# Layer two's first weight loads: one slot handed back two products sooner, one load that waits for rows instead of their stores, one slot freed at the next turn

## The chip, the cores and the metric

The kernel runs on one NeuronCore of a Trainium2 chip. The metric is the device time of one execution in microseconds; the median of three runs is shown, and beside them stands one profiled execution with its trace.

## What is computed

Two layers of a decoder trunk on 520 tokens (512 of a prompt and 8 sampled ones) with a width of 1024, all in float32. Each layer is a mixer, a layer norm, a mixture of experts and another layer norm:

```
xp = layer_norm(ALPHA * xp + mixer(xp))      # layer one: short conv, layer two: RG-LRU
mp = hier_moe(xp, w_group, w_expert, w_gate[32], w_up[32], w_down[32])
xp = layer_norm(ALPHA * xp + mp)
# hier_moe: the best of 4 groups, the best 2 of its 8 experts for each token
hmid = silu(xb @ w_gate[e]) * (xb @ w_up[e]);  out = hmid @ w_down[e]
```

One expert has three weights of 1024 x 512 (2 MB each), so a layer reads 32 x 3 x 2 MB = 192 MB of expert weights.

## The kernel before

**The ring.** All weights pass through `ring`, ten slots of 2 MB. A load is called by its position; `ring_slot` gives its slot, `CYCLE` (line 104) the order of slots in an expert layer. SyncE (`block.sync`) issues all weight loads in the order of their positions, each once TensorE has freed its slot. TensorE says so by counting up one semaphore, `freed`: certain matmuls carry an increment, and because TensorE works in order, the start of such a matmul says that all before it are done. SyncE's `room(pos)` waits for a count. For the first ten loads of an expert layer the counts are written out in `ROOM` (line 106, one tuple for each layer), after that `freed_after` (line 154) gives them. The three slots of expert 0 are handed back in parts (`SPLIT`): the gate weights in two quarters and a half, the up and down weights in two halves.

**The end of the mixer, which the change touches.** The output projection is computed as a two-level sum with seven products for each of four column groups q, numbered i = 1 to 7 (`EARLY`, `LATE`, lines 116 and 117). The last order of them is (q,6), (q,7), (q,4) for q = 0 to 3, then (0,3), (0,2), (1,3), (1,2), (2,3), (2,2), (3,3), (3,2). A product is 4 matmuls in the program and 8 in the trace, since each float32 matmul shows as two. In layer two slot 5 holds the sums of tokens ("pieces") that products 4, 5, 6 and 7 read, slot 6 the copies, slot 7 the sums of weights that the products (q,3) read, slots 3 and 4 the output weights. Between the products stand short products for the router (`logits`, line 889).

In layer two `freed` goes up at product (1,3) (this one after a wait for `zT_done`), at (2,3) and at the last of `logits`. Load 5 (into slot 5) and load 6 wait for the first of these, load 7 for the second, load 8 and load 9 for the last.

**From the mixer to the experts.** Then the rows of tokens are turned and normalized: `turn_token` on TensorE, the scaling on ScalarE (line 1425), which counts up `xn_done` for each of five tiles of 104 tokens. Each tile is stored to `x1_dram`, three by ScalarE's queue (line 1418) and two by GpSimd's (line 666). Expert 0's rows are picked on TensorE from what is in SBUF. Expert 1's rows are gathered from `x1_dram` by an indirect DMA of GpSimd (line 675), which waits for all five stores (`x1_out`, `row_in`); it is the first of the gathers. Load 9 of layer two waits for the same five stores on SyncE (lines 528 and 529), and what SyncE has to issue after it is queued behind it.

**One expert on TensorE** (`expert`): the gate product (`project(0, ...)`), the up product (`project(1, ...)`), half of the turning of the next expert's rows (`turn_rows`, line 1060), the turning of the hidden rows, the other half, and the down product (`down`, line 1143). `project` with `free` counts up `freed` at its first matmul, and for expert 1 that signal frees the second half of expert 0's down slot. Expert 0 turns expert 1's rows (`next_rows(False)`) after its down product, in one piece, and then computes `destinations`.

Of the kernel before, what the change touches and what calls it, by code (L numbers as in the profile page):

```python
# [19 lines left out]
NT = T // TT  # L20
LAST = SEQ - (NT - 1) * TT
HALF = T // 2
DEPTH = 2
# [47 lines left out]
POS_EXP = (POS_OUT[0] + U_OUT, POS_OUT[1] + U_OUT)  # L71
# [14 lines left out]
SPLIT = [p + u for p in POS_EXP for u in range(3)]  # L86
# [16 lines left out]
DENSE = U_IN[0] + U_OUT  # L103
CYCLE = ((2, 3, 4, 5, 6, 7, 0, 1, 8, 9), (0, 1, 8, 9, 2, 5, 6, 3, 4, 7))
SCRATCH = ((0, 1), (5, 6, 7))
ROOM = ((6, 6, 6, 6, 6, 6, 8, 8, 9, 10), (1, 2, 3, 4, 5, 6, 6, 7, 8, 8))


def ring_slot(pos):

    if pos < DENSE:
        return pos
    l = int(pos >= POS_EXP[1])
    return CYCLE[l][(pos - POS_EXP[l]) % RING]
# [13 lines left out]
def late_at(n):  # L128

    return len(EARLY) + n  # L130
# [22 lines left out]

def freed_after(pos):

    return pos + 1 + sum(pos >= p for p in SPLIT) + sum(pos >= p for p in POS_EXP) + int(pos >= POS_EXP[1])


def gathered(e):
# [14 lines left out]
def room_count(pos):  # L174

    for l in range(DEPTH):
        if POS_EXP[l] <= pos < POS_EXP[l] + RING:
            return (0, freed_after(POS_IN[1] - 1))[l] + ROOM[l][pos - POS_EXP[l]]
    return freed_after(pos - RING)
# [7 lines left out]
def build(nc, a, outs):  # L187
    y_prompt, y_sample, na_p, na_s, nb_p, nb_s, nh_p, nh_s = outs
    with ExitStack() as ctx:
# [3 lines left out]
        def sem(name):  # L193
            return ctx.enter_context(nc.semaphore(name))
# [174 lines left out]
        row_in = sem("row_in")  # L369
# [14 lines left out]
        mm_gate = sem("mm_gate")  # L384
# [26 lines left out]
        xn_done = sem("xn_done")  # L411
        x1_out = sem("x1_out")
# [89 lines left out]
        def _(sp):  # L502
# [5 lines left out]
            def expert(l, pos, e):  # L508
                for u, w in enumerate((gates, ups, downs)):
                    s = ring_slot(pos + u)  # L510
                    if pos + u - RING in SPLIT:
                        half = KT * FE // 2
                        if pos + u - RING in POS_EXP:
                            sp.wait_ge(freed, freed_after(pos + u - RING) - 2)
                            sp.dma_start(ring[:, s, :half // 2], w[l][e][:, :half // 2]).then_inc(loaded[s], 16)
                            sp.wait_ge(freed, freed_after(pos + u - RING) - 1)
                            sp.dma_start(ring[:, s, half // 2:half], w[l][e][:, half // 2:half]).then_inc(loaded[s], 16)
                        else:
                            sp.wait_ge(freed, freed_after(pos + u - RING) - 1)
                            sp.dma_start(ring[:, s, :half], w[l][e][:, :half] if u < 2 else w[l][e][:, 0, :]  # L520
                                         ).then_inc(loaded[s], 16)
                        room(pos + u)
                        sp.dma_start(ring[:, s, half:], w[l][e][:, half:] if u < 2 else w[l][e][:, 1, :]
                                     ).then_inc(loaded[s], 16)
                        continue
                    room(pos + u)
                    if pos + u == POS_EXP[1] + RING - 1:
                        sp.wait_ge(x1_out, 16 * 2 * DEPTH)
                        sp.wait_ge(row_in, 16 * (13 + 3 * DEPTH))
                    out = ring[:, s, :] if u < 2 else ring[:, s, :].rearrange("p (h n) -> p h n", h=2)  # L530
                    if e == END and u > 0:
                        half = KT * FE // 2
                        first, second = ((w[l][e][:, :half], w[l][e][:, half:]) if u == 1
                                         else (w[l][e][:, 0, :], w[l][e][:, 1, :]))
                        sp.dma_start(ring[:, s, :half], first).then_inc((last_up, last_down)[u - 1], 16)
                        sp.dma_start(ring[:, s, half:], second).then_inc(loaded[s], 16)
                        continue
                    sp.dma_start(out, w[l][e]).then_inc(loaded[s], 16)
# [29 lines left out]
            for l in L:  # L568
# [4 lines left out]
                else:  # L573
# [3 lines left out]
                    pos = POS_IN[1] + KT // 2  # L577
# [6 lines left out]
                for u in range(U_OUT):  # L584
                    pos = POS_OUT[l] + u
# [18 lines left out]
                with sp.If(n_over > 0):  # L604
                    sp.wait_ge(y_mm[l], END)
                    with sp.Fori(0, n_over) as o:
                        sp.wait_ge(v_y[l], o + 1)
                        e = sp.value_load(over_i[0:1, bass.ds(o, 1)], min_val=0, max_val=NE - 1)
# [127 lines left out]
        def _(pe):  # L736
# [111 lines left out]
            for l in L:  # L848
# [30 lines left out]
                q = 2 * l  # L879
# [85 lines left out]
                for n in range(3, len(LATE)):  # L965
                    q, i = LATE[n]
                    bank_free(late_at(n))
                    late_sum(q, i)
                    free = 0
                    if (q, i) == (1, 3):  # L970
                        pe.wait_ge(zT_done, KT * l + KT // 2)
                        free = (2, 1)[l]
                    if (q, i) == (2, 3):
                        free = 1
                    out_product(l, q, i, late_at(n), free=free).then_inc(out_mm, 1)
                    if q and i == 7:
                        logits(q - 1)
                    if i == 2:
                        logits(KT // 2 + q - 1)
# [114 lines left out]
                def project(u, slot, free, first=False, split=False, halves=False):  # L1094

                    for k in range(KT):
                        if halves:
                            half_in(last_up, 1, k, KT)
                        if first and k == KT // 2:
                            row_numbers()  # L1100
                        if first and k in (0, 2):
                            pe.wait_ge(t_sb[l], k // 2 + 1)
                        if first and k == KT // 2:
                            pe.wait_ge(t_dve, l + 1)
                        for hf in range(2):
                            col = k * FE + hf * FH
                            mm = pe.matmul(ps[hf * ROWS:(hf + 1) * ROWS, (GATE_BANK, 3)[u], :FH],  # L1107
                                           xgT[:, k, :], ring[:, slot, col:col + FH],
                                           start=(k == 0), stop=(k == KT - 1))
                            if free and (k, hf) in (((1, 1), (KT // 2 - 1, 1)) if first else ((0, 0),)):  # L1110
                                mm.then_inc(freed, 1)
                            if split and (k, hf) == (KT // 2 - 1, 1):
                                mm.then_inc(freed, 1)
                    return mm
# [35 lines left out]
                def expert(e, sums_too=False):  # L1150

                    pos = POS_EXP[l] + 3 * e
                    slots = [ring_slot(pos + u) for u in range(3)]
                    if e > 0:
                        pe.wait_ge(t_sb[l], e + 2)
                    pe.wait_ge(loaded[slots[0]], load_target(pos))
                    project(0, slots[0], True, first=(e == 0)).then_inc(mm_gate, 1)
                    if e < END:
                        pe.wait_ge(loaded[slots[1]], load_target(pos + 1))
                    b = (e + 1) % IN_BUFS  # L1160
                    project(1, slots[1], True, split=(e == 0), halves=(e == END)).then_inc(gu_mm[l], 1)

                    def next_rows(free, ks=range(KT)):
                        pe.wait_ge(gath[IN_BUFS * l + b], gathered(e + 1))
                        turn_rows(xg[b], t_mm[l], free, ks)

                    if e + 1 in CHOSEN:
                        choose_rows(e + 1)
                    elif 0 < e < END:
                        next_rows(True, range(KT // 2))  # L1170
                    if sums_too:
                        overflow_rows()
                    if e == 0:
                        pe.wait_ge(idx_ok[l], 1)
                        state_rows()
                    pe.wait_ge(hid_ok[l], e + 1)
                    turn_hidden(h_mm[l], e in (0, END))
                    if e + 1 in CHOSEN:
                        turn_chosen(e + 1)
                    elif 0 < e < END:  # L1180
                        next_rows(False, range(KT // 2, KT))
                    if e < END:
                        pe.wait_ge(loaded[slots[2]], load_target(pos + 2))
                    pe.wait_ge(h_sb[l], e + 1)
                    pe.wait_ge(y_act[l], e)
                    down(slots[2], y_mm[l], split=(e == 0), halves=(e == END))
                    if e == 0:
                        pe.wait_ge(st_sb, 2 * (l + 1))
                        next_rows(False)
                        destinations()  # L1190

                def turn_end():
# [1039 lines left out]
```

## Time and profile before

| | us |
|---|---|
| median of 3 runs | 1406.62 |
| lowest and highest | 1405.63 and 1407.18 |
| profiled execution | 1409.14 |
| its span | 1407.4 |

| engine | busy us | share of the span |
|---|---|---|
| TensorE matmul | 1346.2 | 96% |
| TensorE weight load | 898.0 | 64% |
| VectorE | 546.6 | 39% |
| ScalarE | 220.0 | 16% |
| GpSimd | 122.2 | 9% |

The granted clock of TensorE is at its full level nearly throughout (0.996 of it as a mean). The DMA engines moved 472.88 MB with a mean of 336 GB/s. In the page's 40 slices of 35.2 us their busy share is 9 tenths and more from slice 8 to 19 and from slice 28 to 39, the two expert layers, and 1 to 3 tenths between them. A busy TensorE is not one at its peak, since ends of matmuls are modelled; a wait on a row is read from the bracket behind it, which has the idle time and what ended it.

### The profile page before, as it was taken

The page shows a single profiled execution, that of the slowest core. Times are in us where ns is not written, and L with a number is a line of the kernel's source. Part 1 is how long each engine was busy: PE and PEld are TensorE (multiplying, and loading weights), DVE is VectorE, ACT ScalarE, POOL GpSimd, SP SyncE. Part 2 cuts the span into 40 slices and gives each one's busy share as a digit, 9 for nine tenths or more (in the row PEclk, how much of TensorE's full clock was granted, in tenths as well). Part 3 has the DMA queues.
Part 4 walks back from the last instruction along what each step waited for, and adds up shares of the span by engine and source line. Part 5 has one row for each costly group of instructions (what it writes and reads, how often), then busy time and mean ns, then how long its engine had stood idle before and what let it go on. Part 6 is the DMA issues. An engine that isn't in the chain of part 4 may idle for free.

```text
span 1407.4 us, 20418 instructions
## 1 busy us (share of the span) xinstructions
PE 1346.2 (96%) x8720; PEld 898.0 (64%) x8720; DVE 546.6 (39%) x1163; ACT 220.0 (16%) x388; POOL 122.2 (9%) x138
## 2 busy tenths in 40 slices
PE   7999999999999999998899999999999999999886
PEld 6888876565555555664478888666555555566452
DVE  5667676322111121232255888652211111213117
ACT  1000014000101000100134444220000001010012
POOL 0000000101100010111010000010001100112100
PEclk9999999999999999999999999999999999999999
DMA  9930178999999999999994113689999999999995
GB/s 265 299 128 1 52 307 336 386 423 427 424 422 425 425 424 421 426 423 422 382 322 153 60 61 120 273 352 425 424 425 422 424 426 424 425 423 423 421 404 215
DMA packets 98892, 472.88 MB, mean 336 GB/s; under 512 B 16669, under 2 KB 51485, under 8 KB 64233
## 3 DMA queue, kind: packets, MB, share of 16 engines
q1 hardware_dynamic: 82797, 449.74, 79.0%
q0 software_dynamic: 11520, 15.52, 3.2%
q10 hardware_dynamic: 4484, 6.30, 1.6%
q8 instruction: 70, 1.15, 0.3%
q14 instruction: 21, 0.17, 0.0%
HBM read 468.77 MB, written 27.32 MB: 352 GB/s over the span
## 4 chain that ended last, share of the span: by engine, by line
PE 82%; DMA 13%; ACT 2%; DVE 2%; issue 1%; SPq 0%; POOL 0%; POOLq 0%; DVEq 0%
PE ps L1107 26%; PE ps L1143 14%; PE ps L799 10%; PE ps L740 9%; PE ps L843 7%; PE ps L1072 7%; DMA ring<-in_moe_w_down 3%; DMA ring<-in_moe_w_up 3%; DMA ring<-in_moe_w_gate 3%; PE ps L1060 3%; DMA yrows<-A,Bt 1%; PE ps L1083 1%; DMA ring<-in_a_w_in 1%; PE ps L1131 1%; PE ps L860 1%
## 5 line engine op out<-in xcount | busy, mean ns | idle before, releaser
L1107 PE MATMUL ps<-ring,A 128*64 128x256 f32 x4096 | 457.0, 380 | 20.1 <-DMA ring<-in_moe_w_up 8.6
L1107 PEld LDWEIGHTS ps<-ring,A 128*64 128x64 f32 x4096 | 324.7, 137 | 163.0 <-issue 43.4
L1143 PE MATMUL ps<-ring,A 128*64 128x512 f32 x1024 | 233.8, 597 | 8.1 <-DMA ring<-in_moe_w_down 1.5
L2077 DVE TENSOR_TENSOR A<-A,ps 128x256 f32<-128x256 f32 x64 | 26.9, 421 | 547.8 <-PE ps L1107 547.8
L1143 PEld LDWEIGHTS ps<-ring,A 128*64 128x64 f32 x1024 | 75.9, 136 | 120.5 <-issue 113.0
L740 PE MATMUL ps<-A,ring 128*128 128x260 f32 x576 | 130.6, 388 | 3.6 <-DMA ring<-in_a_w_in 3.6
L740 PEld LDWEIGHTS ps<-A,ring 128*128 128x128 f32 x576 | 111.2, 193 | 21.2 <-issue 3.8
L675 POOL DMA_INDIRECT A<-x,idx x42 | 44.5, 1060 | 678.7 <-PE ps L1060 628.9
L1072 PE MATMUL ps<-C,Bt 104*64 104x512 f32 x400 | 95.6, 620 | 0.0
L2080 DVE COPY A<-ps 128x256 f32<-128x256 f32 x64 | 27.1, 424 | 120.6 <-PE ps L1131 120.6
L1480 ACT ACTIVATE A<-ps 128x512 f32<-128x512 f32 x42 | 25.1, 597 | 307.2 <-PE ps L1143 307.2
L1072 PEld LDWEIGHTS ps<-C,Bt 104*64 104x64 f32 x400 | 34.1, 135 | 47.8 <-issue 46.1
L799 PE MATMUL ps<-A,ring 128*128 128x260 f32 x264 | 61.6, 382 | 0.0
L843 PE MATMUL ps<-ring 128*128 128x260 f32 x256 | 58.0, 385 | 0.0
L1060 PE MATMUL ps<-ident,A 128*128 128x128 f32 x336 | 55.2, 288 | 1.2 <-DMA A<-x,idx 1.2
L1060 PEld LDWEIGHTS ps<-ident,A 128*128 128x128 f32 x336 | 44.3, 195 | 18.3 <-issue 18.3
L1467 ACT ACTIVATE A<-ps 128x256 f32<-128x256 f32 x64 | 24.5, 383 | 200.2 <-PE ps L1107 198.0
L799 PEld LDWEIGHTS ps<-A,ring 128*128 128x128 f32 x264 | 50.2, 190 | 7.7
L843 PEld LDWEIGHTS ps<-ring 128*128 128x128 f32 x256 | 48.1, 190 | 9.6 <-issue 2.5
L682 POOL DMA_INDIRECT yrows<-A,Bt x42 | 44.3, 1055 | 91.6 <-ACT A L1480 83.6
L843 PE MATMUL ps<-Bt,ring 128*128 128x260 f32 x192 | 44.3, 386 | 0.0
L843 PEld LDWEIGHTS ps<-Bt,ring 128*128 128x128 f32 x192 | 36.0, 190 | 7.7 <-issue 2.5
(300 smaller groups left out, 1160.2 us busy)
## 6 DMA issues: line engine op xcount, KB each, us to landing
ring<-in_moe_w_gate SPq DMA_DIRECT2D x62, 2048.0 KB, 25.9
ring<-in_moe_w_up SPq DMA_DIRECT2D x60, 2048.0 KB, 25.7
ring<-in_moe_w_down SPq DMA_DIRECT2D x60, 2048.0 KB, 29.0
ring<-in_a_w_in SPq DMA_DIRECT2D x24, 512.0 KB, 7.6
ring<-yrows SPq DMA_DIRECT2D x10, 1024.0 KB, 9.1
ring<-in_moe_w_down SPq DMA_DIRECT2D x8, 1024.0 KB, 35.8
ring<-in_b_w_in SPq DMA_DIRECT2D x8, 1024.0 KB, 12.8
ring<-in_moe_w_up SPq DMA_DIRECT2D x6, 1024.0 KB, 37.7
```

The costliest lines, as they stand in the source:

```text
L675: pool.indirect_dma_start(out=xg[e % IN_BUFS], out_offset=None, in_=x1_dram[l], in_offset=bass.IndirectOffsetOnAxis(ap=idx[:, e:e + 1], ax ...
L682: pool.indirect_dma_start(out=half_rows, out_offset=bass.IndirectOffsetOnAxis(ap=where, axis=0), in_=rows, in_offset=None, bounds_check=2 ...
L740: mm = pe.matmul(bank, lhs(k), rhs(k), start=(k == 0), stop=(k == KT - 1))
L799: mm = pe.matmul(ps[:, part_bank(u, i), :HALF], w[:, k, :], x[i][:, k, :] if i in x else pieces[4 * t[i] + k], start=(k == 0), stop=(k == ...
L843: mm = pe.matmul(ps[:, out_bank(l, g), :HALF], w[:, k, :], x(k), start=(k == 0), stop=(k == KH - 1))
L1060: mm = pe.transpose(ps[:, k // 4, (k % 4) * P:(k % 4 + 1) * P], xv[:, k, :], ident[:, :])
L1072: mm = pe.matmul(ps[h * ROWS:(h + 1) * ROWS, 7, :], slots1[:, i, :], xv[:, h], start=(i == 0), stop=(i == NT - 1))
L1107: mm = pe.matmul(ps[hf * ROWS:(hf + 1) * ROWS, (GATE_BANK, 3)[u], :FH], xgT[:, k, :], ring[:, slot, col:col + FH], start=(k == 0), stop=(k ...
L1143: mm = pe.matmul(ps[nh * ROWS:(nh + 1) * ROWS, 2, :], hidT[:, at:at + ROWS], ring[:, slot, m * D + nh * 512:m * D + (nh + 1) * 512], start ...
L1480: act.activation(yo[j], ps[:, 2, :], ACT.Copy).then_inc(y_act[l], 1)
L2077: tt(gated, gated, ps[:, 3, :FH], ALU.mult).then_inc(ready, 1)
L2080: dve.tensor_copy(hidT, ps[:, 4, :FT * ROWS]).then_inc(ready, 1)
```

## The change

It moves signals and waits, and adds or removes no computation and no transfer.

1. In layer two, product (0,3) counts up `freed` as well. The counts of `ROOM` behind it and `freed_after` go up by one, so that load 5 waits for (0,3) and all others for what they waited for.
2. Load 9 of layer two waits until all five tiles are normalized in that layer (`xn_done` at 15) instead of for their stores.
3. In both layers, expert 1's gate product no longer counts up `freed`; the first transpose of expert 1's rows, at the end of expert 0, does.

```diff
-ROOM = ((6, 6, 6, 6, 6, 6, 8, 8, 9, 10), (1, 2, 3, 4, 5, 6, 6, 7, 8, 8))
+ROOM = ((6, 6, 6, 6, 6, 6, 8, 8, 9, 10), (1, 2, 3, 4, 5, 6, 7, 8, 9, 9))
...
-    return pos + 1 + sum(pos >= p for p in SPLIT) + sum(pos >= p for p in POS_EXP) + int(pos >= POS_EXP[1])
+    return pos + 1 + sum(pos >= p for p in SPLIT) + sum(pos >= p for p in POS_EXP) + 2 * int(pos >= POS_EXP[1])
...
                     if pos + u == POS_EXP[1] + RING - 1:
-                        sp.wait_ge(x1_out, 16 * 2 * DEPTH)
-                        sp.wait_ge(row_in, 16 * (13 + 3 * DEPTH))
+                        sp.wait_ge(xn_done, NT * (2 * DEPTH - 1))
...
-                    if (q, i) == (2, 3):
+                    if (q, i) == (2, 3) or (l, q, i) == (1, 0, 3):
                         free = 1
...
-                    project(0, slots[0], True, first=(e == 0)).then_inc(mm_gate, 1)
+                    project(0, slots[0], e != 1, first=(e == 0)).then_inc(mm_gate, 1)
...
                     if e == 0:
                         pe.wait_ge(st_sb, 2 * (l + 1))
-                        next_rows(False)
+                        next_rows(True)
                         destinations()
```

## Rows read from the trace of the kernel before

**Rows 1.** The chain of waits: start us, us, what
```profile
630.55 42.39 DMA ring<-in_moe_w_up
...
1264.41 36.79 DMA ring<-in_moe_w_gate
1301.20 42.65 DMA ring<-in_moe_w_down
...
1373.38 7.05 DMA ring<-yrows
```

**Rows 2.** Stretches: us, busy of each engine, clock, DMA share, GB/s
```profile
910.00:913.00 3.00, 3.00 (x14) 0.92 (x16) 2.69 (x10) 2.07 (x2) 0.57 (x1) 1.00 0.92 313
913.00:916.00 3.00, 2.92 (x18) 1.30 (x14) 2.23 (x8) 0.95 (x3) 0.00 (x0) 1.00 0.94 277
916.00:919.00 3.00, 2.45 (x52) 1.83 (x54) 2.87 (x9) 2.95 (x8) 0.00 (x0) 1.00 0.57 193
919.00:922.00 3.00, 3.00 (x43) 2.07 (x38) 2.65 (x14) 1.52 (x3) 0.12 (x1) 1.00 0.07 26
...
1020.00:1300.00 280.00, 276.14 (x1938) 162.59 (x1936) 57.34 (x104) 26.18 (x51) 34.81 (x33) 1.00 1.01 424
```

**Rows 3.** Timeline of SyncE's queue, layer two: start us, us, the issue
```profile
889.20 0.38 SPq L538 DMA_DIRECT2D ring<-in_moe_w_down  x1
...
902.03 0.38 SPq L538 DMA_DIRECT2D ring<-in_moe_w_down  x1
921.10 0.33 SPq L538 DMA_DIRECT2D ring<-in_moe_w_gate  x1
...
933.35 0.33 SPq L523 DMA_DIRECT2D ring<-in_moe_w_gate  x1
936.80 0.33 SPq L538 DMA_DIRECT2D ring<-in_moe_w_up  x1
```

**Rows 4.** Waits of SyncE's queue: us in total, times, longest us
```profile
SPq L529 <- DMA x<-C: 18.6, 1, 18.6
```

**Rows 5.** Issues at 936.80: count, KB, us to landing
```profile
ring<-in_moe_w_up SPq DMA_DIRECT2D x1, 2048.0 KB, 14.7
```

**Rows 6.** Issues at 260.78, the twin in layer one
```profile
ring<-in_moe_w_up SPq DMA_DIRECT2D x1, 2048.0 KB, 7.6
```

**Rows 7.** Timeline of TensorE, layer two: start us, us, group
```profile
884.30 3.67 PE L843 MATMUL ps<-Bt,ring 128*128 128x260 f32 x16
...
888.46 3.77 PE L843 MATMUL ps<-Bt,ring 128*128 128x260 f32 x16
...
929.97 1.13 PE L1060 MATMUL ps<-ident,A 128*128 128x128 f32 x8
...
932.67 7.13 PE L1107 MATMUL ps<-ring,A 128*64 128x256 f32 x64 [0.27 <-DVE A L2051]
```

**Rows 8.** DMA queues from 910 to 913: packets, MB, share of 16 engines
```profile
q10 hardware_dynamic: 132, 0.49, 44.6%
q1 hardware_dynamic: 45, 0.25, 25.1%
q0 software_dynamic: 64, 0.19, 21.2%
```

**Rows 9.** Timeline of ScalarE, the last tile normalized in layer two
```profile
910.86 1.22 ACT L1425 ACTIVATE C<-ps,stat 104x1024 f32<-104x1024 f32 x1
```

**Rows 10.** Issues of expert 1's gather in layer two, at 921.88
```profile
A<-x,idx POOLq DMA_INDIRECT x1, 8.0
```

**Rows 11.** Expert 1's gather in layer one, and TensorE behind it
```profile
A<-x,idx POOLq DMA_INDIRECT x1, 8.9
...
253.97 1.13 PE L1060 MATMUL ps<-ident,A 128*128 128x128 f32 x8 [1.24 <-DMA A<-x,idx]
```

**Rows 12.** Issue at 657.98 and its landing: layer one's last half
```profile
657.98 3.35 SPq L536 DMA_DIRECT2D ring<-in_moe_w_down  x1
...
ring<-in_moe_w_down SPq DMA_DIRECT2D x1, 1024.0 KB, 35.6
```

**Rows 13.** Issue at 1339.46 and its landing: layer two's last half
```profile
1339.46 4.41 SPq L536 DMA_DIRECT2D ring<-in_moe_w_down  x1
...
ring<-in_moe_w_down SPq DMA_DIRECT2D x1, 1024.0 KB, 36.0
```

**Rows 14.** The store of GpSimd's queue issued at 911.27
```profile
x<-C POOLq DMA_DIRECT2D x1, 416.0 KB, 9.3
```

## The prediction

> **What bounds the kernel now.** I read the chain of waits first. Each of the two expert layers ends in a stretch where TensorE is waiting for weights: "DMA ring<-in_moe_w_up" holds 42.39 us of layer one, and two weight loads hold 36.79 and 42.65 us of layer two, after which comes the fetch of the scattered rows [rows 1]. Then I read busy time and DMA by stretch: from 1020 to 1300 us the sixteen DMA engines are at 1.01 with 424 GB/s, and TensorE is at 276 of 280 us [rows 2]. So TensorE works off what the ring of ten slots holds until it meets the DMA stream, and the end of an expert layer comes when the last of 192 MB of weights has landed. A microsecond is won or lost only where that stream has a hole or fills one. In layer two the hole is at its start: the DMA share falls to 0.57 and 0.07 in 916 to 922 us [rows 2]. The issues on SyncE's queue and its waits say why: the tenth load of the ring goes out at 921.10, after an 18.6 us wait for the stores of the normalized rows [rows 3, 4]. From there the stream has a backlog. The second expert layer's load issued at 936.80 (expert 4's up weights; I call it load 13, counted from 0 in its layer) needs 14.7 us to land [rows 3, 5]; its twin in layer one, issued at 260.78, needs 7.6 us [rows 6]. The difference, 7.1 us, is the backlog in layer two at that point, and its most possible gain if every byte had moved earlier.
>
> The sums are made in the profiled execution (1409.14 us, span 1407.4); its own time is 2.5 us over the median of the three runs, and I carry the difference over to the median 1406.62.
>
> **Part 1, slot 5 handed back at product (0,3).** Load 5 goes out at 889.20, right after product (1,3) begins at 888.46; (0,3) begins at 884.30 [rows 3, 7]. So load 5 goes out near 885.0, 4.2 us sooner. Loads 6 and 7 keep their products, because the raised counts only take in the new signal. Load 8 waits for the last logits product and stays at 902.03 [rows 3]. Three loads at 424 GB/s [rows 2] take 3 x 4.95 us, so the first three are through at about 901 instead of 905, the queue runs empty, and load 8, issued at 902.03, has ended by about 908.5. TensorE waits for none of them. What the part brings is that the stores no longer share with the tail of load 8: SyncE's queue (q1) holds 25.1% of the engines in 910 to 913 [rows 8], which is 0.75 us of work. That is its whole worth to the stream.
>
> **Part 2, load 9 waits for the normalized rows, not for their stores.** ScalarE ends the last of them at 910.86 + 1.22 = 912.08 [rows 9], so load 9 goes out at about 912.2, 8.9 us sooner. If nothing else moved, it would fill the idle time of the DMA engines from 913 to 922, where the first bytes of the old load 9 flow: 0.06 x 3 + 0.43 x 3 + 0.93 x 3 = 4.3 us [rows 2], with the 0.75 us of part 1 5.0 us in all. That is the upper end.
> Against it stands what the old wait protected. The stores, 5 of 416 KB, are in their queues from 910 to 921, and expert 1's gather waits for the last: it goes out at 921.88, lands after 8.0 us at 929.9, and TensorE turns its rows at 929.97 with no idle time shown [rows 7, 10]. There is no slack. In layer one the gather lands late and TensorE idles 1.24 us [rows 11]. So each microsecond by which the last store lands later is one by which TensorE starts expert 1 later, and everything that TensorE frees afterwards (load 13's slot half-way through the up and gate products, and so on) is issued later by as much. Call it d. The trace shows no store beside a load of 16 KB rows, so I bound it. Load 9 is 2048 KB, 4.95 us of all engines. Off go 0.75 us (part 1), and up to 1.3 us of idle in 916 to 919 (0.43 x 3); on go the two quarters of load 10, which no longer stand behind load 9's issue and go out when project's first products free them, at about 917.6 and 918.5: 2 x 512 KB, 0 to 2.5 us of which come ahead of the last store. d lies between 4.95 - 0.75 - 1.3 = 2.9 and 4.95 - 0.75 + 2.5 = 6.7 us. I take the middle, 4.8, because half of the idle is a tail of few engines and half of the quarters should slip in.
> What d leaves: load 13 is issued at 936.80 + 4.8 = 941.6. Work ahead of it, counted from 913.3: loads 9 to 12, 19.8 us; stores left, 4.3 us; gathers and state rows, about 3.4 us (an estimate: from 922 to load 13's landing at 951.5 are 29.5 us, five loads are 24.75 of them, and 1.3 is half of what an unloaded load takes beyond its 4.95). That ends at 941, and load 13's bytes start 1.3 us after its issue, at 942.9, so there is no backlog left, and load 13 lands as its twin does, 7.6 us after issue, at 949.2: 2.3 us sooner than 951.5. In formula: gain at load 13 = 7.1 - d, at most 5.0. One more term: a stream that starts without backlog has small holes among its next loads. Layer one's, from load 13's landing at 268.4 to the last half at 657.98 + 35.6 = 693.6, takes 425.2 us; layer two's, from 951.5 to 1339.46 + 36.0 = 1375.5, takes 424.0 [rows 5, 6, 12, 13]. So 1.2 us is given back. Part 2 and 1 together: 7.1 - 4.8 - 1.2 = 1.1 us gained.
>
> **Part 3, the second half of expert 0's down slot freed at the next turn.** No instruction is added; the signal moves from expert 1's first gate product (932.67) to the first transpose of its rows (929.97) [rows 7], 2.7 us. On SyncE that one issue (933.35 [rows 3]) comes sooner and nothing is queued before it. The issue after it is unmoved, since load 13 waits for expert 1's up products. In layer two before, 7.1 us of backlog cover it: nothing. After, with d = 4.8 it goes out at 935.4 and flows from 936.7, and the work ahead of it ends near 938.3: no hole. Without part 3 it would flow from 939.5 to 942.0, which is still ahead of load 13's first bytes: nothing again, and up to 1.2 us if d is much smaller. In layer one TensorE frees at 253.97 + 0.3 instead of 256.7, but load 13's twin stays at 260.78 and already lands in the 7.6 us of an unloaded queue, so nothing follows: 0, bounded by -0.3 (it shares with a gather that has 4 us to spare and more) and +0.4.
>
> Sum: -1.1 us, all of it in layer two. Forecast 1406.62 - 1.1 = 1405.5.
>
> Weighed against a rule: in layer two the two classes of packets that share an engine in 910 to 913 split it about as 25 to 66 [rows 8], and this says nothing about the order within an engine. The Trainium skill, "DMA: Bandwidth & Descriptors", section on queues, rings and completion order, says that an engine goes round the queues that have work and drains a whole packet of some 9 to 17 descriptors from one before it moves on. By that, load 9's share on an engine would go in one piece ahead of the remaining stores; the rows cannot show that, and it speaks against the change. The mechanism is rival B.
>
> **Rivals.**
> A. The stores are hardly held up: load 9 fills only what the stores leave idle (d of 2.1 or less). For it: 0.57 and 0.07 share [rows 2]; against it: in 910 to 916 the share is 0.92 to 0.94, and the stores' packets lie in just that stretch. Time: 1406.62 - 5.0 + up to 0.6 = 1402.0.
> B. Loads go ahead of the stores in whole pieces: load 9 and both quarters of load 10 in full, d = 6.7. For it: a store of 416 KB takes 9.3 us from issue to landing even without a load beside it [rows 14], so it is easily overtaken. Time: 1406.62 - (7.1 - 6.7 - 1.2) = 1407.4.
> C. The other side: the gather is hit twice. The last store lands 7.45 us late (load 9 and quarters), and the gather itself, whose latency is 8.0 us in layer two and 8.9 in layer one [rows 10, 11], finds load 10's second half and part of load 11 ahead of it, another 0.9 to 2.5 us. d = 9.9, gain 7.1 - 9.9 - 1.2 = -4.0: 1410.6. From d = 5.9 on the change is a loss; from 8.7 on one that can be measured. Against it: the gather waits in the same full queue before as well.
> D. The stream's lead does not reach the end, because TensorE becomes the bound: 1406.6. Against it are 79 us of weight waits late in the chain [rows 1].
>
> **How the numbers follow.** A difference under 0.2% (2.8 us) cannot be told from none. Forecast (d from 2.9 to 5.9) 0.50, A 0.18, B 0.15, C 0.09, D 0.08. The forecast's own range is 1403.6 to 1406.6. For the 8 in 10, I take A's side down to 1402.3 and C's up to 1408.6. Faster by over 0.2% needs d under 3.1: A and a sliver of the forecast, 0.21. Slower by over 0.2%: C, less a part that stays under it, 0.08. Same: 0.71.
>
> **What would show it.** Right: load 5 issued near 885, load 9 near 912.2 with no stretch of 913 to 922 at low share; expert 1's gather issued at 925 to 928 and TensorE idle 3 to 6 us before it turns those rows; load 13 landing in some 8 us instead of 14.7; the last weight half landing some 1 us sooner; layer one unmoved. Wrong: a gather still issued by 924 (A), load 13 issued after 945 (C), or a final weight landing that moves without the span moving (D).

## The result, and the profile after

| | median us | runs | ratio to before, 95% interval |
|---|---|---|---|
| before | 1406.83 | 17 | |
| changed | 1411.12 (1407.61 to 1416.63) | 17 | 1.0029 [1.0019, 1.0039] |

The change makes the kernel 4.3 us slower (interval 2.7 to 5.5); the forecast was 1.1 us faster. The profiled execution has a span of 1411.8 us against 1407.4, 4.4 us more, with a mean granted clock of 0.990 against 0.996. In it all work ahead of the change lies 0.37 us earlier than before (product (0,3) at 883.93 against 884.30), which has to be added when its times are held against those of before.

SyncE's queue in layer two of the changed kernel (start us, us, issue) answers to [rows 3]:

```profile
884.56 0.38 SPq L537 DMA_DIRECT2D ring<-in_moe_w_down  x1
...
901.66 0.38 SPq L537 DMA_DIRECT2D ring<-in_moe_w_down  x1
911.77 0.33 SPq L537 DMA_DIRECT2D ring<-in_moe_w_gate  x1
917.29 0.33 SPq L515 DMA_DIRECT2D ring<-in_moe_w_up  x1
918.15 0.33 SPq L517 DMA_DIRECT2D ring<-in_moe_w_up  x1
...
934.83 0.33 SPq L523 DMA_DIRECT2D ring<-in_moe_w_gate  x1
944.79 0.33 SPq L537 DMA_DIRECT2D ring<-in_moe_w_up  x1
```

Loads 5 and 9 go out where they were forecast (885 and 912), but load 13 goes out at 944.79 instead of 941.6. Its landing (changed kernel, issue at 944.79: KB, us to landing) is the unloaded 7.7 us that the forecast had:

```profile
ring<-in_moe_w_up SPq DMA_DIRECT2D x1, 2048.0 KB, 7.7
```

The stretches show that the hole at 916 to 922, which stands in [rows 2], is filled. A new one has opened at 941 to 945, where nothing is loaded. The third figure from the end of each row is the granted clock of TensorE:

```profile
910.00:913.00 3.00, 3.00 (x16) 0.99 (x14) 2.69 (x10) 1.70 (x2) 0.57 (x1) 1.00 0.92 264
913.00:916.00 3.00, 2.54 (x16) 1.16 (x12) 2.21 (x9) 1.33 (x5) 0.00 (x0) 1.00 0.99 264
916.00:919.00 3.00, 2.82 (x58) 2.16 (x60) 2.90 (x10) 2.95 (x7) 0.00 (x0) 1.00 0.92 360
919.00:922.00 3.00, 3.00 (x30) 1.99 (x29) 2.62 (x15) 1.14 (x3) 0.00 (x0) 1.00 0.96 397
...
930.00:934.00 4.00, 0.00 (x0) 0.00 (x0) 0.00 (x0) 0.28 (x1) 0.00 (x0) 0.85 1.04 425
934.00:936.00 2.00, 1.65 (x8) 1.57 (x8) 0.00 (x0) 0.00 (x0) 0.00 (x0) 0.50 0.74 264
934.00:944.00 10.00, 9.65 (x80) 6.98 (x82) 7.14 (x22) 0.00 (x0) 0.99 (x1) 0.55 0.47 172
941.00:945.00 4.00, 4.00 (x30) 2.42 (x28) 3.31 (x9) 0.39 (x1) 0.00 (x0) 0.74 0.00 0
```

The gather of expert 1's rows on GpSimd, and TensorE around it, answer to [rows 7, 10] (in brackets the idle time before a group and what ended it):

```profile
926.35 1.08 POOL L674 DMA_INDIRECT A<-x,idx  x1 [14.88 <-DMA x<-C]
```

```profile
925.99 3.65 PE L1142 MATMUL ps<-ring,A 128*64 128x512 f32 x16 [0.56 <-issue]
934.35 1.95 PE L1059 MATMUL ps<-ident,A 128*128 128x128 f32 x8 [4.71 <-DMA A<-x,idx]
936.23 2.35 PE L1042 MATMUL ps<-Bt 104*64 104x32 f32 x40
938.38 9.40 PE L1106 MATMUL ps<-ring,A 128*64 128x256 f32 x64
```

Here the loss arises. The gather goes out 926.35 + 0.37 - 921.88 = 4.8 us later, and TensorE turns its rows 4.75 us later, after 4.71 us of idle time. In that idle time the granted clock falls from 2.4 to 1.2 GHz (0.85 as a mean of 930 to 934, 0.50 from 934 to 936, 0.55 as a mean of 934 to 944), so the same 8 transposes take 1.95 us instead of 1.13, and expert 1's 64 gate and up matmuls 9.40 instead of 7.13. Load 13's issue is 8.0 + 0.37 = 8.4 us late: 4.75 from the gather, 1.33 up to the start of expert 1's gate product, 2.28 up to its up product, these last two, 3.6 us, from the clock. The forecast's formula then holds: 7.1 - 8.4 = -1.3 at load 13, and by the rows load 13 lands at 952.5 + 0.37 against 951.5.

The last half of the weights (issue and, of that issue, KB and us to landing) lands at 1342.31 + 36.0 = 1378.3 against 1375.5 [rows 13]:

```profile
1342.31 4.30 SPq L535 DMA_DIRECT2D ring<-in_moe_w_down  x1
```

That is 2.8 us, or 3.2 with the 0.37 added: 1.4 from load 13 and 1.8 from the stream behind it (425.8 against 424.0 us). Another 1.6 us of the span come at the very end. In the chains of waits the first matmuls that sum up the scattered rows are, in the changed kernel:

```profile
1383.32 3.66 PE ps L1244 x4
```

and in the kernel before:

```profile
1380.47 1.96 PE ps L1245 x4
```

The granted clock of the changed kernel from 1380 to 1390 is 0.83:

```profile
1380.00:1390.00 10.00, 8.27 (x21) 2.49 (x18) 8.45 (x13) 2.55 (x5) 0.00 (x0) 0.83 1.00 422
```

TensorE waits for the scattered rows there in both kernels. In this one execution the clock fell there, in that of before it did not. The same sums at the end of layer one, which the change leaves alone, show such a fall in three of the experiments' profiled executions (3.2 to 3.7 us instead of 1.96) and none in the others. In the kernel kept busy, which stands below, behind a wait of only 1.02 us:

```profile
698.80 3.48 PE L1246 MATMUL ps<-ring,Bt 104*104 104x512 f32 x4 [1.02 <-DMA ring<-yrows]
```

So this fall depends on the execution. The 17 runs of the changed kernel have mean clocks from 0.988 (1416.63 us) to 0.994 (1407.61 us); the correlation of clock and time is -0.87.

### The profile page after: what moved, and what is told of

Its sections match the earlier page's. It is cut to its first block, busy times and chain, and to the rows that moved or that the text cites. A ratio compares the mean times of both kernels' runs of the same rounds, so it can differ in the third digit from the quotient of the medians.

```text
span 1411.8 us, 20418 instructions
## 1 busy us (share of the span) xinstructions
PE 1350.5 (96%) x8720; PEld 901.6 (64%) x8720; DVE 546.7 (39%) x1163; ACT 220.0 (16%) x388; POOL 122.2 (9%) x138
## 4 chain that ended last, share of the span: by engine, by line
PE 83%; DMA 12%; ACT 2%; DVE 2%; issue 1%; SPq 0%; POOL 0%; POOLq 0%; DVEq 0%
PE ps L1106 27%; PE ps L1142 14%; PE ps L798 10%; PE ps L739 9%; PE ps L842 7%; PE ps L1071 7%; DMA ring<-in_moe_w_down 3%; DMA ring<-in_moe_w_up 3%; PE ps L1059 3%; DMA x<-C 2%; DMA A<-x,idx 1%; DMA yrows<-A,Bt 1%; PE ps L1130 1%; PE ps L1082 1%; PE ps L1244 1%
```

## The experiments

Each kernel was timed against before on the same chip. Medians are in us, and the brackets behind a ratio are its 95% interval. A time in a profiled execution is put "on before's scale" by the difference in the work ahead of the change, as the 0.37 us above.

**Part 2 alone.** Before, with only the wait of load 9 exchanged:

```diff
-                        sp.wait_ge(x1_out, 16 * 2 * DEPTH)
-                        sp.wait_ge(row_in, 16 * (13 + 3 * DEPTH))
+                        sp.wait_ge(xn_done, NT * (2 * DEPTH - 1))
```

> Only part 2 of the change (load 9 of layer two waits for normalized rows, not their stores). Theory T: part 2 alone makes the loss. Load 9 runs beside the stores, expert 1's gather goes out near 926, TensorE idles 4 to 6 us before it turns the rows, and in that idle time its granted clock falls from 2.4 to 1.2 GHz for about 10 us, which costs another 3.5 to 4 us. Expected 3 to 6 us slower than before, as the full change (4.3 us slower). Rival R (parts 1 or 3 do the harm, by signals that move the order of loads): this kernel within 1.5 us of before.

Measured: 1411.84 (7 runs), ratio 1.0029 [1.0013, 1.0045]. The profiled execution is the fastest of the seven (1407.06), and its work ahead of the change lies 4.2 us earlier than that of before. On before's scale its gather goes out 5.2 us late and its rows are turned 5.0 us late. TensorE idles before the turn and takes 1.95 us for it:

```profile
930.79 1.95 PE L1059 MATMUL ps<-ident,A 128*128 128x128 f32 x8 [4.94 <-DMA A<-x,idx]
932.66 2.35 PE L1042 MATMUL ps<-Bt 104*64 104x32 f32 x40
```

Part 2 by itself is enough for a loss of this size.

**Parts 1 and 3 alone.** The change, with the old wait of load 9 put back (the diff above, reversed).

> The change without part 2 (slot 5 handed back at product (0,3), second half of the first down slot freed at the next turn; load 9 waits for the stores again). Theory T: no wait for the gather in layer two, load 5 issued near 885, load 13 landing as before, within 1 us of before. Rival R: 2 us and more slower.

Measured: 1405.13, ratio 0.9985 [0.9975, 0.9995]. That these parts do the harm is excluded. Their gain of 2.3 us is more than the 1 us that I had expected at most, but the interval (0.7 to 3.5) holds 1. Added to the 4.4 us of part 2 alone it gives 2.1 us of loss, not the 4.3 of the whole; the intervals are wide enough for this, so it does not show that the parts act on each other. In its profile, the issue of load 13 (KB, us to landing) still meets a backlog:

```profile
ring<-in_moe_w_up SPq DMA_DIRECT2D x1, 2048.0 KB, 12.7
```

and what releases the gather is not a store but VectorE's row numbers, for which line 675 waits as well:

```profile
920.49 1.08 POOL L675 DMA_INDIRECT A<-x,idx  x1 [8.98 <-DVE idx L1550]
```

**The change, with TensorE kept busy.**

```diff
                         pe.wait_ge(st_sb, 2 * (l + 1))
+                        if l == 1:
+                            warm(16, 3)
                         next_rows(True)
```

`warm(16, 3)` issues 16 matmuls of the identity whose result nothing reads.

> The full change, with 16 extra matmuls of 128 columns of the identity into a free PSUM bank on TensorE in layer two, ahead of its wait for expert 1's gathered rows; they hold TensorE for about 4.2 us. Theory T: the gather is as late (issue near 926, rows turned near 934.4), but the granted clock stays at 2.4 GHz, the first group of expert 1's gate and up products takes 7.1 us instead of 9.4, load 13 goes out near 941.5 instead of 944.8, and the time is 3 to 4 us below the full change, so within 2 us of before and as the prediction had it. Rival L (only the lateness of the gather counts, the clock is a by-product that the weight stream hides): the time stays within 1 us of the full change, 3 to 5 us above before.

Measured: 1408.78, ratio 1.0013 [1.0000, 1.0026]; the full change had 1411.12. TensorE in its profile:

```profile
930.48 3.84 PE L763 MATMUL ps<-ident 128*128 128x128 f32 x32
934.16 1.05 PE L1059 MATMUL ps<-ident,A 128*128 128x128 f32 x8
935.14 1.36 PE L1042 MATMUL ps<-Bt 104*64 104x32 f32 x40
936.77 7.13 PE L1106 MATMUL ps<-ring,A 128*64 128x256 f32 x64 [0.28 <-DVE A L2052]
```

and the clock, third from the end:

```profile
934.00:938.00 4.00, 3.73 (x63) 3.13 (x64) 2.52 (x9) 0.00 (x0) 0.99 (x1) 1.00 0.99 387
```

Work that computes nothing takes 2.3 us out of the loss, with the clock at 1.00 and the 64 matmuls at 7.13 us. That speaks for the clock as a cost of its own and against rival L. The size is uncertain, since the intervals of the two ratios overlap. And the profiled execution (span 1406.6, its work 0.54 us later than before's ahead of the change) is not the full change with the clock alone put right, because its gather is less late:

```profile
925.39 1.08 POOL L674 DMA_INDIRECT A<-x,idx  x1 [13.01 <-DMA x<-C]
```

That is 3.0 us late on before's scale instead of 4.8, though nothing ahead of it was edited. The rows landed at 933.2, before the added matmuls ended at 934.3, so here these held the turn up by about 1 us. Load 13 goes out at 940.90 and lands 8.8 us later, at 949.2 on before's scale against 951.5. The forecast had this gain of 2.3 us, but from a wait of 4.8 us and a landing of 7.6, so that the two agree by chance. Four of the twelve runs have a clock of 0.992 or 0.993 and take 1410.5 to 1413.7 us, the others 1405.5 to 1409.3. Where the clock fell in those four no trace shows.

**Load 9 in two early halves.** Load 9 keeps out of the stores' way. Part 2's wait goes, parts 1 and 3 stay. The second half of load 9 only needs the products (q,7) to be done.

```diff
@@ behind load 5
+                    if pos + u == POS_EXP[1] + 5:
+                        half, s9 = KT * FE // 2, ring_slot(POS_EXP[1] + RING - 1)
+                        sp.dma_start(ring[:, s9, half:], gates[l][3][:, half:]).then_inc(loaded[s9], 16)
@@ load 9
                     if pos + u == POS_EXP[1] + RING - 1:
-                        sp.wait_ge(xn_done, NT * (2 * DEPTH - 1))
+                        half = KT * FE // 2
+                        sp.dma_start(ring[:, s, :half], w[l][e][:, :half]).then_inc(loaded[s], 16)
+                        continue
@@ unit_dmas
+    if pos == POS_EXP[1] + RING - 1:
+        return 2
```

> The full change, but load 9 in two halves that are out of the stores' way: its second half (whose place in slot 7 is read only by the products (q,7)) is issued right behind load 5 at product (0,3), its first half right behind load 8 at the last logits product; it waits for no rows. Theory T: the stores share only some 0.7 us with loads, expert 1's gather is issued by 922.5, TensorE idles at most 1.5 us as in layer one, the clock stays at 2.4 GHz, load 13 lands about 8 us after its issue near 937, and the time is 3 to 5 us under before. Rival S (a backlog in front of load 13 is worth nothing, the end is set elsewhere): within 1 us of before.

Measured: 1403.39 (7 runs), ratio 0.9968 [0.9956, 0.9979], which beats both kernels. The issues of load 5, the two halves and load 13:

```profile
883.73 0.38 SPq L541 DMA_DIRECT2D ring<-in_moe_w_down  x1
884.15 0.47 SPq L544 DMA_DIRECT2D ring<-in_moe_w_gate  x1
...
901.26 0.47 SPq L531 DMA_DIRECT2D ring<-in_moe_w_gate  x1
...
937.08 0.33 SPq L541 DMA_DIRECT2D ring<-in_moe_w_up  x1
```

and TensorE's wait for the gather, behind which the clock did not fall:

```profile
930.26 1.13 PE L1066 MATMUL ps<-ident,A 128*128 128x128 f32 x8 [1.44 <-DMA A<-x,idx]
```

The gather goes out when it did before (920.73 + 1.19 on before's scale, against 921.88), but takes 9.4 us to land instead of 8.0, hence the wait. The backlog is worth its microseconds if it is removed without holding up the stores.

**Part 1 alone.** Parts 1 and 3 without the diff's last two hunks.

> Part 1 alone: slot 5 of layer two handed back at product (0,3), all else as before. Parts 1 and 3 together were 2.3 us faster than before in the last runs. Theory E (the weight queue is empty when the stores begin, so the stores, the gather and load 9 all come about 1 us sooner): this kernel has nearly all of it, 1.5 to 2.5 us under before, the wait for the stores ending 1 us sooner after the mixer's end. Rival N (part 1 is worth 0.75 us at most, as predicted, and part 3 the rest): within 0.8 us of before.

Measured: 1406.29, ratio 0.9996 [0.9984, 1.0007]. The median lies between the two expectations, and the interval reaches into both.

**A late gather with no store beside a load.** Parts 1 and 3, and on GpSimd the gather held back until load 9 has landed:

```diff
                 pool.wait_ge(idx_ok[l], 1)
+                if l == 1:
+                    late = POS_EXP[1] + RING - 1
+                    pool.wait_ge(loaded[ring_slot(late)], load_target(late))
```

> Parts 1 and 3, load 9 behind the stores as before, and expert 1's gather in layer two held back on GpSimd until load 9 has landed (near 927). So the gather is as late as in the full change or a little later, yet no store ever ran beside a load. Theory T: TensorE idles 5 to 7 us, its clock falls to 1.2 GHz for 7 to 10 us, and the time is 4 to 7 us above parts 1 and 3 alone, in spite of the backlog of 7 us in front of load 13. Rival B (what costs is the mixing of stores and loads on the DMA engines, and the backlog hides TensorE's delay): at most 1.5 us above parts 1 and 3 alone.

Measured: 1411.35, ratio 1.0025 [1.0015, 1.0035]. That is 6.2 us over parts 1 and 3, or 5.6 by the two ratios, which were measured at different times. Its TensorE and its clock are those of the changed kernel:

```profile
934.41 1.94 PE L1063 MATMUL ps<-ident,A 128*128 128x128 f32 x8 [5.11 <-DMA A<-x,idx]
936.28 2.35 PE L1046 MATMUL ps<-Bt 104*64 104x32 f32 x40
938.43 9.04 PE L1110 MATMUL ps<-ring,A 128*64 128x256 f32 x64
```

```profile
934.00:938.00 4.00, 3.59 (x40) 3.29 (x42) 1.54 (x4) 0.00 (x0) 0.87 (x1) 0.50 1.02 420
```

The lateness of one gather is enough; rival B of this expectation (not the prediction's B), that the mixing costs and the backlog covers the delay, falls.

**Halves, and destinations ahead of the turn.**

```diff
-                        next_rows(True)
                         destinations()
+                        next_rows(True)
```

> Load 9 in two early halves as before, and in both layers TensorE computes the sums of destinations (1.4 us) ahead of turning expert 1's gathered rows instead of behind it. Theory T: TensorE's delay sets load 13 there, since it lands 8 us after its issue with no backlog; the 1.4 us wait for the gather shrinks to nearly nothing, and load 13 goes out about 1.3 us sooner: 0.5 to 1.5 us under the kernel with halves alone (1403.4). Rival: VectorE gets the turned rows no sooner and the gate product of expert 1 waits as long: no change, or up to 1.3 us slower where the gather has already landed.

Measured: 1404.49 (1402.94 to 1411.25), ratio 0.9984 [0.9971, 0.9996]. No better than the halves alone; the gain did not appear in the median, and one run of 1411.25 had a clock of 0.991. The times are inconclusive. The profile speaks for the rival, for TensorE no longer waits for the gather, but expert 1's gate product waits for VectorE, 1.56 us instead of 0.27:

```profile
931.57 7.13 PE L1113 MATMUL ps<-ring,A 128*64 128x256 f32 x64 [1.56 <-DVE A L2057]
```

On before's scale it starts at 933.8, against 934.1 with the halves alone: 0.3 us of the 1.3 expected.

**Load 10 held back until the stores have landed.** The change, and behind the issue of load 9 a wait that holds load 10 and all after it:

```diff
+                    if pos + u == POS_EXP[1] + RING - 1:
+                        sp.wait_ge(x1_out, 16 * 2 * DEPTH)
+                        sp.wait_ge(row_in, 16 * (13 + 3 * DEPTH))
```

> The full change, but load 10 of layer two (whose two first quarters go out near 917.5 and 918.4 beside the stores) waits on SyncE until all stores have landed. It tells what load 9 does to the stores by itself. Theory T1 (load 9's 4.95 us are what holds the stores): the gather goes out within 1 us of the full change's 926.35, TensorE idles over 3.5 us, the clock still falls in most runs, and the time stays 3 us and more above before. Rival Q (the quarters make half of it): the gather goes out by 924.5, TensorE idles under 3 us, and the time is within 2 us of before.

Measured: 1411.01, ratio 1.0028 [1.0015, 1.0042], and the gather's issue:

```profile
927.20 1.08 POOL L677 DMA_INDIRECT A<-x,idx  x1 [14.97 <-DMA x<-C]
```

Its work lies 0.39 us later than before's ahead of the change, so the gather is 4.9 us late with load 9 alone beside the stores. None of what rival Q expected came, and it falls. That the quarters of load 10 add nothing at all is not shown: it is one execution of each kernel, and the gather of one and the same code was 4.8 us late in one and 3.0 in another (the kernel kept busy). The gather takes 8.8 us to land here, and TensorE idles 5.71 us.

**Half the dose.** The change, with load 9's second half behind the stores (and load 9 counted as two transfers, as in the halves):

```diff
+                        half = KT * FE // 2
+                        sp.dma_start(ring[:, s, :half], w[l][e][:, :half]).then_inc(loaded[s], 16)
+                        sp.wait_ge(x1_out, 16 * 2 * DEPTH)
+                        sp.wait_ge(row_in, 16 * (13 + 3 * DEPTH))
+                        sp.dma_start(ring[:, s, half:], w[l][e][:, half:]).then_inc(loaded[s], 16)
+                        continue
```

> The full change with half the dose: load 9's first half (1 MB) goes out when the rows are normalized, its second half after the stores. Theory T: the stores are held up half as long, the gather goes out 2 to 3 us sooner than in the full change (near 924), TensorE idles 2 to 3 us, too short in most runs for its clock to fall, and the time is near the forecast for the full change: 1405 to 1408. Rival L (lateness and clock scale with the dose): half of the loss, 1409 to 1410, with a granted clock between that of before (0.995) and of the change (0.991).

Measured: 1408.06, ratio 1.0005 [0.9995, 1.0015], with a mean clock over its runs of 0.995, as before's. It is nearer to theory T: half the load beside the stores costs 0.7 us by the ratio, where half of the full loss would be 2.1, which is the end of the interval. In its profiled run, the slowest of the twelve, TensorE idles 2.09 us before the turn, and the clock was lower in part of what followed (0.61 from 938 to 942), so even here it falls at times:

```profile
935.91 1.14 PE L1067 MATMUL ps<-ident,A 128*128 128x128 f32 x8 [2.09 <-DMA A<-x,idx]
...
938.61 8.36 PE L1114 MATMUL ps<-ring,A 128*64 128x256 f32 x64
```

```profile
938.00:942.00 4.00, 4.00 (x34) 2.61 (x34) 3.69 (x15) 0.00 (x0) 0.83 (x1) 0.61 1.01 420
```

Most of this run's length comes from layer one, which the halves of load 9 do not touch. There the clock fell as well, in the wait for the same gather, and the work ahead of the change in layer two lies 3.8 us later than before's:

```profile
255.10 1.94 PE L1067 MATMUL ps<-ident,A 128*128 128x128 f32 x8 [2.23 <-DMA A<-x,idx]
```

With the 3.8 us taken off, layer two's gather goes out 2.6 us late (928.30), about half of what the whole load cost it.

**Part 3 alone.** The diff's last two hunks on the kernel before.

> Part 3 alone: the second half of expert 0's down slot freed at the first transpose of expert 1's rows. Parts 1 and 3 together were 2.3 us faster, part 1 alone 1.0 us with an interval that holds nothing. If part 3 fills a hole of the weight stream in layer one (where load 13 meets an unloaded queue), this is 0.5 to 1.5 us faster than before; if it is worth nothing, as predicted, within 0.5 us of before, and load 13 of layer one still lands 7 to 8 us after an issue that has not moved.

Measured: 1406.80, ratio 1.0001 [0.9990, 1.0012]: nothing, as predicted. That load 13 of layer one would keep its issue and its landing was not met: it goes out at 259.14 instead of 260.78, since TensorE did not wait for the gather of layer one in this execution, and takes 9.8 us to land instead of 7.6. No time follows from that. In layer two, up to the gather, this kernel is that of before, and yet the gather's last release is not a store:

```profile
921.13 1.08 POOL L675 DMA_INDIRECT A<-x,idx  x1 [8.97 <-DVE idx L1550]
```

On before's scale it goes out at 920.8, as with parts 1 and 3 and with part 1 alone, and load 9 at 919.8 against 921.1. So the stores of one and the same code end more than a microsecond apart from one execution to another.

## Why the prediction was wrong

**The step that failed** is in part 2: "each microsecond by which the last store lands later is one by which TensorE starts expert 1 later, and everything that TensorE frees afterwards ... is issued later by as much". That priced idle time of TensorE at its own length. It costs more: in 4.7 us of idle time the clock falls to 1.2 GHz, and the matmuls of the next 10 us take 3.6 us more up to the release of load 13. With it the sum is 7.1 - 4.8 - 3.6 - 1.2 = -2.5, a loss of 2.5 us in place of 1.1 us of gain; 3.2 were read at the last weight, on before's scale. Keeping TensorE busy gave 2.3 us back, a late gather by itself cost about 6. The Trainium skill, "TensorE: Matmul & The Clock Gate", section "HAM oscillation — how this bites in real kernels", tells of just this: a wait for a DMA between two pieces of matmul work, after which TensorE starts at its low clock. The trace agrees, with 0.50 behind the wait. I had weighed a rule on DMA queues, which changed little, and not this one, which speaks against an edit that makes TensorE wait for a DMA between its matmuls.

**What held.** The chain's reading (the end moves with the weight stream) held in both directions: a start of expert 1 that was 5.1 us late cost about 6 us, and the halves gained 4.1. TensorE's delay was taken as 4.8 us from bounds of 2.9 and 6.7, and was 4.75 in the profiled execution. The backlog of 7.1 us, the filled hole of 916 to 922, the unloaded landing of 7.7 us and the loss behind an empty queue (1.2 forecast, 1.8 measured) held too.

**The size of d was met in part by luck.** The middle of d was the sum of four terms: load 9's own 4.95 us, less the work that part 1 takes away, less half of the idle time of 916 to 919, plus half of the quarters. With load 10 held, which takes the last term away, the gather was still 4.9 us late; with part 2 alone, which takes the second away, 5.2. That looks like load 9's own time and nothing else. But with the same code up to the gather, the kernel kept busy had 3.0, the lower bound. Single executions differ by as much as the terms are worth, so which of them holds stays open, and that 4.8 was met so well is luck. The reading "there is no slack" was also one execution's: the gather waits for VectorE's row numbers too, and these are there at 920.8 on before's scale, 1.1 us ahead of the last store in the profile of before. In that of part 3 alone the stores came first.

**Part 1 may have been taken as too small.** Parts 1 and 3 together gained 2.3 us, interval 0.7 to 3.5, where 0.75 were allowed. That is just inside, part 3 alone is nothing, and part 1 alone is 1.0 with an interval that holds nothing, so how much part 1 is worth is open. With parts 1 and 3, load 9 goes out 1.9 us sooner (918.89 and 0.33 of offset against 921.10), but 1.3 us sooner with part 3 alone too, which moves nothing there.

**The rivals.** B gave d as 6.7, with load 9 and both quarters ahead of the stores in whole pieces. The measured delays are 3.0 to 5.2 us, and B's time of 1407.4 is 3.7 us off. Whether load 9 itself went ahead in one piece is neither confirmed nor excluded. C had the right side and nearly the time (1410.6) by another mechanism: stores 7.45 us late and a gather whose own latency grows. In the changed kernel it did not grow: 7.9 us against 8.0 (9.4 with the halves, 8.8 with load 10 held). A and D fell. The chance of a slower kernel, 0.08, was too low because the mechanism that made it slower was not among those weighed.

**The end.** That the clock fell in the last sums of the profiled execution is not shown to be an effect of the change, since it falls in such sums at the end of layer one too. The medians carry 4.3 us, of which the stream explains 3.2 in the one execution that has a profile. Whether the rest is the spread of the clock among runs stays open.

## What to carry to other kernels

A wait that an edit adds to TensorE, or lengthens by microseconds, is priced as its length and what the lower clock takes in the work behind it, here 4.7 us and 3.6 more. Before a transfer is sent sooner, look at what shares the DMA engines then and who waits for that one: in the kernel before, load 9 landed at 929.2 and TensorE needed it at 957.1; sent sooner, it held up stores that had nothing to spare in that execution. And where a load is to fill a hole, the better place may be an earlier hole: with half a slot that was free sooner the same idea gained 4.1 us (interval 3.0 to 6.2). A single profile can mislead on terms of a microsecond or two: stores, gathers and clock differed by that much between executions of the same code.

## What the runs showed of the hardware

A load of 2 MB issued beside stores of 416 KB delayed the last of the five by about its whole own time in three of four executions; that time is 4.95 us at 424 GB/s. The gather that waits for it went out 4.8 us late with two quarter loads behind, 4.9 us late without, 5.2 with part 2 alone, and 3.0 in one more execution; with half the load it was 2.6. The load itself needed 13.5 us to land (issue at 911.77: KB, us to landing) instead of 8.1 before, so both sides were slowed:

```profile
ring<-in_moe_w_gate SPq DMA_DIRECT2D x1, 2048.0 KB, 13.5
```

The granted clock fell in or behind every idle time of TensorE of 4.7 us and more that the traces have before these transposes: 4.71 us in the changed kernel, 4.94, 5.11 and 5.71 in three others. With shorter ones it depends on the execution. It fell with 2.09 and 2.23 us (half the dose, layers two and one), and with waits of 1.0 to 1.3 us at the end of layer one in three executions. It did not fall with 1.44 us (halves), with 1.24 us in layer one [rows 11], nor with 2.48 us in layer one of the changed kernel, whose transposes take the full clock's 1.1 us. In the 2.09 us case the transposes behind the wait still had the full clock (1.14 us), and the fall came about 2 us into the work. The length of the wait in front of the work does not settle it by itself:

```profile
254.02 1.13 PE L1059 MATMUL ps<-ident,A 128*128 128x128 f32 x8 [2.48 <-DMA A<-x,idx]
```
